# Recurrence gates in rounded terms with splits made early, and attention scores issued two parts at a time with tiles turned back four steps behind

## The chip, the cores and the metric

The kernel runs on 1 core of one Trainium2 chip. The metric is the time of one execution on the device, in microseconds. A core has TensorE (PE, with its weight loads as PEld), VectorE (DVE), ScalarE (ACT), GpSimd (POOL) and SyncE (SP); each takes its instructions in the order of its own queue, and semaphores tie the queues together.

## What is computed

Three transformer layers over 512 tokens of 1024 features: a hybrid of 8-head sliding-window attention and an RWKV recurrence, a sparse attention of 16 heads with three branches, and a block of dilated attention beside an LRU recurrence; each with feed-forward layers around it. What the change touches is this of the reference:

```python
# sliding window, 8 heads: band of two 128-key blocks, a sink per head
p = jnp.exp(s - m); p = p / (jnp.sum(p, -1, keepdims=True) + jnp.exp(sink - m))
# sparse attention, 16 heads: three branches, each a softmax of its own, summed under gates
return g_blk[..., 0, None] * o_cmp + g_blk[..., 1, None] * o_slc + g_blk[..., 2, None] * o_win
# LRU: two gates from the convolved input xc, per head of 256 channels
gate_x = jax.nn.sigmoid(jnp.einsum('bshi,hij->bshj', xh, w_x) + b_x)
gate_a = jax.nn.sigmoid(jnp.einsum('bshi,hij->bshj', xh, w_a) + b_a)
```

## The kernel before, in words

**Products.** Activations lie as features x tokens, 8 tiles of 128x512. Weights come in units of 8 blocks of 128x128 (one unit is one output tile of a product over 1024 features) into `raw`, issued by SP as slots come free (`SLOTS` = 6). ScalarE rounds a unit to `w_hi` (L123), VectorE makes the rest, `w_lo` (L130), and TensorE takes three rounded matmuls for each block (L155, L156, L157): high by high, high by low, low by high. Both engines prepare `AHEAD` = 4 units past the tile that they are at, and they do it in their own program order: in each tile of a product stands first the preparation (`act_ahead`, `dve_ahead`), then the tile's own work.

**The xr product and the convolution** (`lru_input`). For each of 8 tiles VectorE evicts the bank to `sq` (L1794), ScalarE makes the first term of a convolution (L1786, semaphore `first`) and VectorE three taps (L1797, `tap1` to `tap3`) into `xc`. Ahead of it, in ScalarE's queue, `load_lru` issues the loads of the gate weights `wx` and `wa` (L2464, L2465, semaphore `loaded`) and of the relative-bias table. After tile 5 TensorE picks relative biases (L1773), and after tile 6's taps VectorE makes the rows `rv` of them (`made`), which ScalarE writes to DRAM at h = 2 (`rel_vectors`).

**The gates** (`Scan`). The next product (`qkv0`, 9 tiles) is a host: ahead of each half tile, h = 0 to 17, stands a piece of other work. Gate t stands at h = 2, 4, .. 14 and 15 (L1851): per gate two weights by two blocks of `xc`, 4 unrounded matmuls of 128x512. Gate 0 shares banks 4 and 5 with tiles 4 and 5 of xr and waits for their eviction, gate 1 for `made`, later gates for the sigmoids of the gate before the last. ScalarE follows with two sigmoids (L1869, L1870), at h = 9 and 16 with powers and tangents (L1856, L1861), GpSimd with a multiplication (L1906), VectorE at h = 11 to 14 with squares (L1894, L1897).

**The attentions** (`paired_attention`) for the 8 heads (swa, 16 parts) and the 16 heads (nsa, 64 parts, two for each group, first the selected and then the local one). A part is scores of two heads, 64 rows each, side by side in the array (L1297), VectorE's bias with minimum (L1306), ScalarE's exponential (L1391), transposes on TensorE (L1317), ScalarE's copy (L1404), and matmuls with the values (L1330). VectorE settles a group (L1440 to L1458) out of its output bank: nsa has two banks, its last step a reduction over three branches (L1458); swa has one, since the recurrence's output (`guest`, L1123 to L1129, with L1143 and L1145 on ScalarE and L1174 to L1181 on GpSimd) takes the other. After four token tiles the finished tile is turned back (L1341), rounded (L1411) and its rest made (L1465). In step p TensorE's queue holds: scores of p + 2, transposes of p, the guest's matmul, value matmuls of p - 1, turning back of p - 2, and at the end an early part of the next product, 12 matmuls a step (L1204 to L1206). The other engines' queues follow the same steps.

## Time and profile before

| | us |
|---|---|
| median of 3 runs | 2758.2 |
| lowest and highest | 2757.69, 2758.71 |
| the profiled execution | 2757.42 |
| its span, first to last instruction | 2755.6 |
| TensorE busy in it | 2711.6 |
| VectorE, ScalarE, GpSimd busy | 1440.7, 1058.5, 36.4 |

The profile page gives busy times, the span in 40 slices, the chain of work that ended last and the costliest groups. The trace gives the single instructions: a row of a timeline has the start in us from the span's start, the duration, the engine, the line of the kernel, the operation, what it writes and reads, the shape, how many rows are merged into it, and in brackets the engine's idle time before it with what ended that. Matmuls overlap, so their cost is the distance between starts.

### The profile page before, as it was taken

The page shows a single profiled execution, that of the slowest core. Times are in us where ns is not written, and L with a number is a line of the kernel's source. Part 1 is how long each engine was busy: PE and PEld are TensorE (multiplying, and loading weights), DVE is VectorE, ACT ScalarE, POOL GpSimd, SP SyncE. Part 2 cuts the span into 40 slices and gives each one's busy share as a digit, 9 for nine tenths or more (in the row PEclk, how much of TensorE's full clock was granted, in tenths as well). Part 3 has the DMA queues.
Part 4 walks back from the last instruction along what each step waited for, and adds up shares of the span by engine and source line. Part 5 has one row for each costly group of instructions (what it writes and reads, how often), then busy time and mean ns, then how long its engine had stood idle before and what let it go on. Part 6 is the DMA issues. An engine that isn't in the chain of part 4 may idle for free.

```text
span 2755.6 us, 38503 instructions
## 1 busy us (share of the span) xinstructions
PE 2711.6 (98%) x16358; PEld 2248.7 (82%) x16358; DVE 1440.7 (52%) x2360; ACT 1058.5 (38%) x1604; POOL 36.4 (1%) x62
## 2 busy tenths in 40 slices
PE   9988999999999999999999999999999999999998
PEld 7787788888887788888888888877888788888887
DVE  6834576643625756756346443274634544654433
ACT  5534454332425654433234222245433422432221
POOL 0000200000000000000000000001000000000000
PEclk9999999999999999999999999999999999999999
DMA  4200122222531002322323332236222232223222
GB/s 161 90 4 3 53 87 98 100 94 98 158 104 39 1 1 100 100 97 95 100 77 107 99 99 93 100 116 129 82 81 87 71 100 98 87 99 99 93 99 69
DMA packets 68686, 238.85 MB, mean 87 GB/s; under 512 B 7800, under 2 KB 10360, under 8 KB 68004
## 3 DMA queue, kind: packets, MB, share of 16 engines
q1 hardware_dynamic: 62256, 220.80, 23.9%
q10 hardware_dynamic: 6260, 15.59, 2.5%
q8 instruction: 130, 2.13, 0.3%
q14 instruction: 40, 0.33, 0.0%
HBM read 228.23 MB, written 6.03 MB: 85 GB/s over the span
## 4 chain that ended last, share of the span: by engine, by line
PE 91%; DVE 4%; ACT 3%; issue 1%; POOL 1%; DMA 0%; ACTq 0%; another core or an unknown queue 0%; DVEq 0%; POOLq 0%
PE psum L155 23%; PE psum L157 23%; PE psum L156 23%; PE psum L1330 3%; PE psum L1297 2%; PE psum L1317 2%; PE psum L843 2%; PE psum L201 2%; PE psum L202 1%; PE psum L209 1%; PE psum L1851 1%; PE psum L177 1%; PE psum L178 1%; PE psum L176 1%; PE psum L1987 1%
## 5 line engine op out<-in xcount | busy, mean ns | idle before, releaser
L155 PE MATMUL psum<-x_hi,w_hi 128*128 128x512 f32 x2128 | 846.1, 398 | 0.7 <-DVE w_lo L130 0.7
L157 PE MATMUL psum<-x_hi,w_lo 128*128 128x512 f32 x2128 | 830.4, 390 | 0.0
L156 PE MATMUL psum<-x_lo,w_hi 128*128 128x512 f32 x2128 | 829.5, 390 | 0.0
L130 DVE TENSOR_TENSOR w_lo<-raw,w_hi 128x1024 fp32r<-128x1024 f32 x409 | 500.2, 1225 | 391.7 <-ACT w_hi L123 391.6
L123 ACT ACTIVATE w_hi<-raw 128x1024 fp32r<-128x1024 f32 x409 | 427.9, 1050 | 306.0 <-DMA raw<-w_down 83.9
L155 PEld LDWEIGHTS psum<-x_hi,w_hi 128*128 128x128 f32 x2128 | 400.0, 188 | 90.6 <-issue 5.7
L156 PEld LDWEIGHTS psum<-x_lo,w_hi 128*128 128x128 f32 x2128 | 400.2, 188 | 85.5 <-issue 5.0
L157 PEld LDWEIGHTS psum<-x_hi,w_lo 128*128 128x128 f32 x2128 | 399.8, 188 | 83.8
L157 PE MATMUL psum<-h_hi,w_lo 128*128 128x512 f32 x616 | 240.0, 390 | 0.0
L156 PE MATMUL psum<-h_lo,w_hi 128*128 128x512 f32 x616 | 240.0, 390 | 0.0
L155 PE MATMUL psum<-h_hi,w_hi 128*128 128x512 f32 x616 | 240.0, 390 | 0.0
L545 ACT ACTIVATE h_hi<-ht 128x512 fp32r<-128x512 f32 x88 | 55.6, 632 | 253.0 <-DVE ht L566 253.0
L157 PEld LDWEIGHTS psum<-h_hi,w_lo 128*128 128x128 f32 x616 | 115.7, 188 | 24.1
L155 PEld LDWEIGHTS psum<-h_hi,w_hi 128*128 128x128 f32 x616 | 115.7, 188 | 23.9
L156 PEld LDWEIGHTS psum<-h_lo,w_hi 128*128 128x128 f32 x616 | 115.7, 188 | 23.7
L553 DVE TENSOR_TENSOR sq<-psum,rn 128x512 f32<-128x512 f32 x88 | 60.7, 690 | 123.6 <-PE psum L157 114.7
L434 ACT ACTIVATE sq<-psum 128x512 f32<-128x512 f32 x49 | 29.2, 595 | 178.0 <-PE psum L157 163.4
L566 DVE TENSOR_TENSOR ht<-ffn_c,psum 128x512 f32<-128x512 f32 x88 | 60.5, 688 | 63.7 <-PE psum L157 61.1
L568 DVE TENSOR_TENSOR h_lo<-ht,h_hi 128x512 fp32r<-128x512 f32 x88 | 61.0, 693 | 61.4 <-ACT h_hi L545 61.4
L201 PE MATMUL psum<-x_hi,w_hi 128*128 128x512 f32 (+1 forms) x248 | 86.1, 361 | 4.8 <-ACT x_hi L286 3.1
L536 ACT ACTIVATE ffn_c<-sq,vec 128x512 f32<-128x512 f32 x44 | 35.9, 815 | 137.7 <-DVE sq L553 137.7
L202 PE MATMUL psum<-x_hi,w_lo 128*128 128x512 f32 (+1 forms) x248 | 83.1, 349 | 0.0
(412 smaller groups left out, 3298.5 us busy)
## 6 DMA issues: line engine op xcount, KB each, us to landing
raw<-w_up SPq DMA_DIRECT2D x88, 512.0 KB, 3.3
raw<-w_down SPq DMA_DIRECT2D x44, 512.0 KB, 3.3
raw<-w_f1up SPq DMA_DIRECT2D x44, 512.0 KB, 3.3
raw<-w_f2up SPq DMA_DIRECT2D x44, 512.0 KB, 3.3
raw<-w_qkv SPq DMA_DIRECT2D x36, 512.0 KB, 3.3
raw<-w_blend SPq DMA_DIRECT2D x28, 512.0 KB, 3.3
raw<-w_f1down SPq DMA_DIRECT2D x22, 512.0 KB, 3.3
raw<-w_f2down SPq DMA_DIRECT2D x22, 512.0 KB, 3.2
```

What stands on the lines that cost most here:

```text
L123: act.activation(self.w_hi[u % SLOTS][:], self.raw[u % SLOTS][:], ACT.Copy).then_inc(self.hi_done, 1)
L130: dve.tensor_tensor(self.w_lo[u % SLOTS][:], self.raw[u % SLOTS][:], self.w_hi[u % SLOTS][:].bitcast(F32), ALU.subtract).then_inc(self.lo_ ...
L155: pe.matmul(bank[:], hi, x_hi[:, kk], start=kk == 0, stop=False)
L156: pe.matmul(bank[:], hi, x_lo[:, kk], start=False, stop=False)
L157: mm = pe.matmul(bank[:], lo, x_hi[:, kk], start=False, stop=kk == kt - 1)
L201: pe.matmul(self.bank(g, t)[:, c], hi, x_hi[:, kk, c], start=n == 0, stop=False)
L202: pe.matmul(self.bank(g, t)[:, c], lo, x_hi[:, kk, c], start=False, stop=False)
L545: act.activation(h_hi[:, p], k.ht[p % 2][:], ACT.Copy).then_inc(high, 1)
L553: dve.tensor_tensor(pre[p % 2][:], gate[:], k.rn[:], ALU.mult).then_inc(k.bank_free, 1)
L566: dve.tensor_tensor(k.ht[p % 2][:], c[p % 2][:], val[:], ALU.mult).then_inc(k.bank_free, 1)
L568: dve.tensor_tensor(h_lo[:, p], k.ht[p % 2][:], h_hi[:, p].bitcast(F32), ALU.subtract).then_inc(low, 1)
L1330: mm = pe.matmul(out_bank[g % len(out_bank)][:, at * V:at * V + w], mem.pt[(c0 + count[(p, c)]) % 4][:, j * P:(j + 1) * P], values, start= ...
```

## The change

The gates: both operands of each gate pair j (gates 2j and 2j + 1) are split. ScalarE rounds the two weights' 128x512 slices (`round_weights`) and the two blocks of `xc` (`round_input`); GpSimd makes the four rests (`remainders`); TensorE multiplies in three rounded terms and waits for the rests (`split_lo`) in place of the load and `tap3`. Pair 0's weights are rounded in tile 0 of xr and its input in tile 2, pair 1's in tiles 3 and 4, pairs 2 and 3 at h = 6 and h = 10. The rounded copies lie in memory that is free at that time (under `acc`, `ln`, `r`, `ht`, `lru_ga`, `lru_gx`, `lru_e` and `z_even`).

The attentions: scores, minima, sink shifts and exponentials of parts p + 2 and p + 3 are both issued in even steps p; tiles are turned back four steps behind instead of two, and the early part of the next product starts one step later. In nsa the reduction over three branches becomes two additions on GpSimd out of a double buffer, and the value matmuls wait for the multiplication that empties the bank, no longer for the reduction.

```diff
+BEHIND = 4
...
-        done = p - 2
+        done = p - BEHIND
...
-                pe.wait_ge(taken, g0 + g + 1 - len(out_bank))
+                if steps == 3:
+                    pe.wait_ge(own, o0 + steps * (g + 1 - len(out_bank)))
+                else:
+                    pe.wait_ge(taken, g0 + g + 1 - len(out_bank))
...
-        for p in range(N + 2):
-            if p + 2 < N:
-                scores(pe, p + 2)
+        for p in range(N + BEHIND):
+            if p % 2 == 0:
+                for q in range(p + 2, min(p + 4, N)):
+                    scores(pe, q)
             if p == 0 and opening:
                 before(pe)
             if p < N:
                 guest.pe(pe, p)
             if 0 <= p - 1 < N:
                 mixes(p - 1)
-            back_to_features(p - 2)
-            if p >= N - 1:
+            back_to_features(p - BEHIND)
+            if p >= N - 4 + BEHIND:
                 head.pe(pe, 2)
...
+    def add_branches(pool, p):
+        g = parts[p].group
+        prod, ob = mem.prod[g % 2], mem.ob[g % 8]
+        pool.wait_ge(own, o0 + steps * g + 3)
+        pool.tensor_tensor(ob[:], prod[:, 0:P], prod[:, P:2 * P], ALU.add).then_inc(paired, 1)
+        pool.wait_ge(paired, g + 1)
+        pool.tensor_tensor(ob[:], ob[:], prod[:, 2 * P:3 * P], ALU.add).then_inc(taken, 1)
+
     def pool(pool):
         if not sinks:
+            for p in range(N):
+                if parts[p].last:
+                    add_branches(pool, p)
...
-                shift_sinks(pool, p + 2)
+        for p in range(N + BEHIND):
+            if p % 2 == 0:
+                for q in range(p + 2, min(p + 4, N)):
+                    shift_sinks(pool, q)
...
+        for p in range(N + BEHIND):
             if p < N:
                 copy(p)
-            features(p - 2)
-            if p + 2 < N:
-                exps(p + 2)
+            features(p - BEHIND)
+            if p % 2 == 0:
+                for q in range(p + 2, min(p + 4, N)):
+                    exps(q)
...
-                dve.tensor_tensor(mem.prod[:].rearrange("p (s v) -> p s v", v=HD), view[:, :, 0:HD],
+                if g >= 2:
+                    dve.wait_ge(taken, g0 + g - 1)
+                dve.tensor_tensor(mem.prod[g % 2][:].rearrange("p (s v) -> p s v", v=HD), view[:, :, 0:HD],
                                   coef.unsqueeze(2).to_broadcast([P, n, HD]), ALU.mult).then_inc(own, 1)
-                dve.wait_ge(own, at + 3)
-                dve.tensor_reduce(mem.ob[g % 8][:].rearrange("p (h v) -> p h v", h=2),
-                                  mem.prod[:].rearrange("p (s h v) -> p h v s", h=2, v=HD), AX.X, ALU.add).then_inc(taken, 1)
...
-                mins(dve, p + 2)
+        for p in range(N + BEHIND):
+            if p % 2 == 0:
+                for q in range(p + 2, min(p + 4, N)):
+                    mins(dve, q)
             if guest:
                 guest.dve(dve, p)
             if 0 <= p - 1 < N:
                 settle(p - 1)
-            lower(p - 2)
+            lower(p - BEHIND)
...
+            early(act, t)
             act.activation(mem.xc[:, t], k.sq[t % 2][:], ACT.Identity, bias=k.v("lconv_b", t),
                            scale=k.v("lconv_w3", t)).then_inc(first, 1)
...
+SPLITS = (6, 10)
...
+    def operands(self, j):
+        k, mem = self.k, self.mem
+        r, e = k.rounded, mem.e_rounded
+        ga, gx = mem.ga_rounded, mem.gx_rounded
+        if j % 2 == 0:
+            return [ga[:, KD - 2], gx[:, KD - 2]], [ga[:, KD - 1], gx[:, KD - 1]], (r[:, 4], r[:, 5])
+        if j == 1:
+            return [ga[:, KD - 4], gx[:, KD - 4]], [ga[:, KD - 3], gx[:, KD - 3]], (r[:, 6], mem.z_rounded[:, 8])
+        return [e[:, 4], e[:, 5]], [r[:, 2], r[:, 3]], (r[:, 6], mem.z_rounded[:, 8])
+
+    def round_weights(self, act, j):
+        mem, (_, _, wh) = self.mem, self.operands(j)
+        if j == 0:
+            act.wait_ge(mem.loaded, 32)
+        if j >= 2:
+            act.wait_ge(self.pair, 2 * j - 2)
+        for hi, w in zip(wh, (mem.wx, mem.wa)):
+            act.activation(hi, w[:, 4 * P * j:4 * P * (j + 1)], ACT.Copy).then_inc(self.w_high, 1)
+
+    def round_input(self, act, j):
+        mem, (xh, _, _) = self.mem, self.operands(j)
+        if j == KD // 2 - 1:
+            act.wait_ge(self.made, 2)
+        act.wait_ge(self.tap3, 2 * j + 2)
+        for kt in range(2):
+            act.activation(xh[kt], mem.xc[:, 2 * j + kt], ACT.Copy).then_inc(self.x_high, 1)
+
+    def remainders(self, pool, j):
+        mem, (xh, xl, wh) = self.mem, self.operands(j)
+        c = slice(4 * P * j, 4 * P * (j + 1))
+        for m, (hi, w, lo) in enumerate(zip(wh, (mem.wx, mem.wa), (mem.wx_lo, mem.wa_lo))):
+            pool.wait_ge(self.w_high, 2 * j + m + 1)
+            pool.tensor_tensor(lo[:, c], w[:, c], hi.bitcast(F32), ALU.subtract).then_inc(self.split_lo, 1)
+        for kt in range(2):
+            pool.wait_ge(self.x_high, 2 * j + kt + 1)
+            pool.tensor_tensor(xl[kt], mem.xc[:, 2 * j + kt], xh[kt].bitcast(F32), ALU.subtract).then_inc(self.split_lo, 1)
+
+    def early(self, act, t):
+        if t in (0, 3):
+            self.round_weights(act, t // 3)
+        if t in (2, 4):
+            self.round_input(act, t // 2 - 1)
...
             if t == 0:
-                pe.wait_ge(mem.loaded, 32)
                 k.tile_kept(pe, self.source, 5)
             if t == 1:
                 pe.wait_ge(self.made, 2)
             if t >= 2:
                 pe.wait_ge(self.ga, t - 1)
-            pe.wait_ge(self.tap3, t // 2 * 2 + 2)
-            for bank, w in zip(self.gate_banks(t), (mem.wx, mem.wa)):
+            j = t // 2
+            xh, xl, wh = self.operands(j)
+            pe.wait_ge(self.split_lo, 4 * j + 4)
+            for bank, hi, w in zip(self.gate_banks(t), wh, (mem.wx_lo, mem.wa_lo)):
                 for kt in range(2):
-                    o = ((t // 2 * 2 + kt) * 2 + t % 2) * P
-                    mm = pe.matmul(bank, w[:, o:o + P], mem.xc[:, t // 2 * 2 + kt], start=kt == 0, stop=kt == 1)
+                    c = slice((kt * 2 + t % 2) * P, (kt * 2 + t % 2 + 1) * P)
+                    low = w[:, 4 * P * j:4 * P * (j + 1)][:, c]
+                    pe.matmul(bank, hi[:, c], xh[kt], start=kt == 0, stop=False)
+                    pe.matmul(bank, hi[:, c], xl[kt], start=False, stop=False)
+                    mm = pe.matmul(bank, low, xh[kt], start=False, stop=kt == 1)
             mm.then_inc(self.pair, 1)
...
+        if h in SPLITS:
+            self.round_weights(act, 2 + SPLITS.index(h))
+            self.round_input(act, 2 + SPLITS.index(h))
...
+        self.remainders(pool, 0)
+        self.remainders(pool, 1)
         for t in range(KD):
+            if t in (3, 5):
+                self.remainders(pool, (t + 1) // 2)
             pool.wait_ge(self.gx, t + 1)
             pool.tensor_tensor(mem.gx[:, t], mem.gx[:, t], mem.xc[:, t], ALU.mult).then_inc(self.b, 1)
```

## Rows read from the trace of the kernel before

**Rows 1.** The page: engine busy (share) xinstructions; granted clock in 40 slices, in tenths.

```profile
PE 2711.6 (98%) x16358; PEld 2248.7 (82%) x16358; DVE 1440.7 (52%) x2360; ACT 1058.5 (38%) x1604; POOL 36.4 (1%) x62
...
PEclk9999999999999999999999999999999999999999
```

**Rows 2.** Timeline of TensorE around gates 0 and 1.

```profile
1848.10 1.88 PE L1851 MATMUL psum<-lru_xc,lru_wx 128*128 128x512 f32 x4
...
1851.76 0.40 PE L156 MATMUL psum<-x_lo,w_hi 128*128 128x512 f32 x1
...
1856.99 1.88 PE L1851 MATMUL psum<-lru_xc,lru_wx 128*128 128x512 f32 x4
```

**Rows 3.** By tile, the load of gate weight wa: start, time from issue to landing.

```profile
L2465 ACTq DMA_DIRECT2D lru_wa<-in_lru_a x1: 491/491/491, 1821.4 to 1821.4; - x1
...
DMA to landing us min/median/max: 12.4/12.4/12.4
```

**Rows 4.** The page, costliest groups: count | busy, mean ns | idle before.

```profile
L545 ACT ACTIVATE h_hi<-ht 128x512 fp32r<-128x512 f32 x88 | 55.6, 632 | 253.0 <-DVE ht L566 253.0
```

**Rows 5.** Timeline of ScalarE and VectorE in tiles 0 to 2 of xr.

```profile
1822.60 0.80 ACT L1786 ACTIVATE lru_xc<-sq,vec 128x512 f32<-128x512 f32 x1
...
1823.43 2.32 DVE L1797 SCALAR_TENSOR_TENSOR lru_xc<-sq,vec,lru_xc 128x511 f32<-128x511 f32 x3 [2.62 <-ACT lru_xc L1786]
...
1825.67 0.69 DVE L1794 TENSOR_TENSOR sq<-psum,rn 128x512 f32<-128x512 f32 x1
...
1829.47 1.22 DVE L130 TENSOR_TENSOR w_lo<-raw,w_hi 128x1024 fp32r<-128x1024 f32 x1
...
1830.61 0.68 DVE L1794 TENSOR_TENSOR sq<-psum,rn 128x512 f32<-128x512 f32 x1
```

**Rows 6.** Timeline, tile 6 on TensorE, the bias rows written, sigmoids of gate 4.

```profile
1831.63 0.50 PE L155 MATMUL psum<-x_hi,w_hi 128*128 128x512 f32 x1
...
1856.83 0.92 ACTq L1874 DMA_DIRECT2D rel_vectors<-rel_rv  x1
...
1885.77 1.06 ACT L123 ACTIVATE w_hi<-raw 128x1024 fp32r<-128x1024 f32 x1 [6.10 <-DMA raw<-w_qkv]
...
1894.46 0.69 ACT L1869 ACTIVATE lru_gx<-psum,vec 128x512 f32<-128x512 f32 x1
```

**Rows 7.** By line, GpSimd's multiplications of 128x512: duration in ns, min/median/max.

```profile
L1906 POOL TENSOR_TENSOR lru_gx<-lru_gx,lru_xc x8: 1277/1406/2277, 1861.1 to 1912.0; 128x512 f32<-128x512 f32 x8
```

**Rows 8.** Timeline, GpSimd and VectorE at the same time.

```profile
1897.33 1.75 POOL L1906 TENSOR_TENSOR lru_gx<-lru_gx,lru_xc 128x512 f32<-128x512 f32 x1 [0.83 <-ACT lru_gx L1869]
...
1897.85 1.78 DVE L1894 SCALAR_TENSOR_TENSOR lru_e<-lru_e,lru_ga 128x512 f32<-128x512 f32 x1
```

**Rows 9.** Timeline of TensorE in nsa, value matmuls ahead of scores and of transposes.

```profile
934.24 1.45 PE L1330 MATMUL psum<-nsa_vt,nsa_pt 128*128 128x65 f32 x12
...
935.62 0.76 PE L1297 MATMUL psum<-nsa_keys,z 64*128 64x287 f32 x4
...
1014.15 1.45 PE L1330 MATMUL psum<-nsa_vt,nsa_pt 128*128 128x65 f32 x12
...
1015.43 0.93 PE L1317 MATMUL psum<-const,nsa_p 128*128 128x128 f32 x7
```

**Rows 10.** By line, the transposes of nsa: duration in ns, min/median/max.

```profile
L1317 PE MATMUL psum<-const,nsa_p x336: 272/273/330, 850.0 to 1016.1; 128*128 128x128 f32 x168
```

**Rows 11.** Timeline, the reduction and the turning back of a tile.

```profile
893.70 0.59 DVE L1458 TENSOR_REDUCE nsa_ob<-nsa_prod 128x128 f32<-128x384 f32 x1
...
894.44 0.63 PE L1341 MATMUL psum<-const,nsa_ob 128*128 128x128 f32 x4 [0.25 <-ACT nsa_pt L1404]
```

**Rows 12.** Stretches, nsa: length, busy (x) of PE, PEld, DVE, ACT, POOL, clock, DMA.

```profile
850.00:1026.00 176.00, 174.26 (x1309) 140.06 (x1310) 118.43 (x506) 115.10 (x297) 0.00 (x0) 1.00 0.02 4
```

**Rows 13.** Timeline, swa: a sink row waited for, the guest waiting for ScalarE.

```profile
283.94 0.20 ACT L1396 ACTIVATE swa_es<-swa_es 128x2 f32<-128x2 f32 x1 [2.54 <-POOL swa_es L1363]
...
287.04 1.13 PE L1129 MATMUL psum<-rw_sg,z 128*128 128x512 f32 x2 [1.55 <-ACT rw_b L1143]
```

27 lines of the change are left out of this document (18 added, 9 removed).

## The prediction

> **What bounds the kernel now.** I read the page first: TensorE is busy for 98% of the span, and the granted clock is at its full level (2.4 GHz) in every slice [rows 1]. So an edit counts only by what it adds to or takes from TensorE's own queue: fewer or shorter matmuls, or a wait that TensorE has to sit out. I then read the timelines of the three places that the change touches. In the recurrence's gates the starts of successive instructions give the price of a matmul: from 1851.76 to 1856.99 lie 23 rounded ones, 0.227 us each, and from 1848.10 to 1851.76 one of these and eight passes of unrounded ones, 0.43 each [rows 2]. Durations don't, since matmuls overlap. In the same place ScalarE and VectorE feed TensorE by an order written out by hand, so their queues count too [rows 3 to 6]. In the two attentions the starts show no idle worth naming between parts, but dearer starts where matmuls of 64 rows begin and end, and one wait per tile turned back [rows 9 to 11].
>
> **Gates: the matmuls.** A gate issues 4 unrounded matmuls, each in two passes: 8 x 0.43 = 3.44 us [rows 2]. The change issues 12 rounded matmuls, 12 x 0.227 = 2.72 us. Eight gates: 8 x 0.71 = **-5.7 us**. Nothing covers or eats this; it is TensorE's own work.
>
> **Gates: the wait for the weights (the main term).** The rounding of the gates' weights now stands in ScalarE's queue in tile 0 of the xr product, ahead of the activation that begins that tile's convolution, and it first waits for both gate weights. Their loads are issued just before, the second at 1821.4, and it lands 12.4 us later, at 1833.8 [rows 3]; until now only TensorE waited for them, at gate 0, and found them there. ScalarE was at that point at 1822.6 [rows 5]. Behind it wait: the activation (L1786), then VectorE's three taps, and behind those in VectorE's queue the low part of weight unit 6 (L130 at 1829.47, ready at 1830.7), which TensorE needs for tile 6 from 1831.63 on [rows 5, 6]. Slack is 0.9 us. New times: loads 1833.8; two roundings, at 0.63 each as L545 [rows 4], 1835.1; first activation 1835.9; taps of 2.24 to 1838.2; eviction, activation and taps of tile 1 to 1842.0; unit 6 ready 1843.1. TensorE stands still some 11.5 us. Then the chain eviction, activation, taps, weight part, which took 4.94 us a tile (1825.67 to 1830.61) [rows 5], gets two roundings more in tiles 2, 3 and 4, 1.25 us each, 6.2 in all against 5.44 for a tile on TensorE (24 x 0.227). It stays in front: tile 5's eviction, which gate 0 needs since it shares its bank, ends at 1843.1 + 3 x 6.2 + 0.7 = 1862.4. Gate 0 starts then instead of at 1848.1: **+14.4 us**. TensorE's own work up to there (tile 6, tile 7 and a hosted tile, 16.3 us) ends at 1859.6, so up to 2.8 us of further slowness of TensorE are hidden here.
>
> The trace of before has no idle of TensorE this long and no half clock to read. The Trainium skill (TensorE: Matmul & The Clock Gate, Part 1) says that an idle TensorE is put back to 1.2 GHz until it has been busy again; nothing here shows it. By rows of the other level, a tile 6 wholly at half clock would take 5.4 us more, of which 2.8 are hidden, so the term is 0 to 2.6, and I take 0.
>
> **Gates: GpSimd beside VectorE.** Sixteen subtractions of 128x512 are new on GpSimd. Eight multiplications of that size took 1.28 to 2.28 there, median 1.41 [rows 7]. VectorE slows beside them: L1894 took 1.78 us where a tap of its size takes 0.75 (three in 2.32) [rows 5], and GpSimd's took 1.75 meanwhile [rows 8]. Four pairs fall into the chain of the last paragraph, and in each the second subtraction lies on VectorE's taps. At up to 1.0 us of VectorE each that is 0 to 4 us (6 if both of a pair meet it); I take three quarters of the one case seen: **+3.0**. The Trainium skill (GPSIMD Engine Reference, Key points) says that GpSimd shares its SBUF interfaces with VectorE instructions of two SBUF inputs; the trace agrees, by the 1.78.
>
> **Gates: two later waits.** Gate 1 needs the relative-bias rows that VectorE makes after tile 6. By the pace of the chain tile 6 was evicted at 1830.61 + 4 x 4.94 = 1850.4 [rows 5], and activation, taps and these rows took some 4.5 more: 1855, 2 us ahead of gate 1. From tile 5's eviction to their end VectorE needs 9.3 us; TensorE now reaches gate 1 only 8.2 after gate 0: **+1.0** (0 to 2). Gate 6 needs the last split. Its roundings stand behind gate 4's sigmoids in ScalarE, and these came only at 1894.46 to 1895.7, because ScalarE had waited until 1885.77 for a weight unit (the write of the bias rows, issued at 1856.83, shares the queues) and then did powers and tangents [rows 6]. One gate and its tile took 8.89 us (1848.10 to 1856.99) [rows 2], so TensorE wanted gate 6 at 1901.4. After: from gate 0's start, the weight unit is issued at +17.3 and lands, as before, some 20 later; sigmoids end at +46.8, GpSimd multiplies (1.3), then four subtractions of 1.3 to 2.0 [rows 7] end at +53 to +56. TensorE wants gate 6 at +50: **+4.5** (0 if the unit lands early, 10 if late and each subtraction takes 2). The split for gates 4 and 5 has 5 us to spare, and the bias loads behind the write may add 0 to 2 later; I take 0.
>
> **Sixteen-head attention (nsa).** The first matmul of 64 rows after the products starts 0.205 instead of 0.112 after the last pass, by which 12 passes take 1.38 ahead of scores and 1.28 ahead of transposes [rows 9]; and the first transpose behind scores takes 0.057 more than the rest, 0.330 against 0.273 [rows 10]. 62 parts come with such a pair of changes; two at a time leaves 31: 31 x 0.15 = **-4.6**. I assume that between two parts' scores no such gap appears (bound: 0 to -4.6). Turning back: L1341 came at 894.44, right behind the reduction that ends at 894.29 [rows 11], where the four passes before it, started at 893.63, would have let it start at 894.03. 7 of 8 tiles show it: 7 x 0.41 = **-2.9**; the last one, behind 4 steps of the early head, waits for nothing, and in its new place it has one step of 2.72 us to cover ScalarE's 0.60 and VectorE's 0.69. The first part's wait of 0.2 is covered too: **-0.1**. Is what feeds TensorE still in time? ScalarE is busy for 115 of 176 us and VectorE for 118 [rows 12]. In the tightest pair (t = 1) ScalarE has 0.60 + 1.06 + 1.41 us after the first transposes and VectorE 1.1 + 1.4; the second scores of the next pair want it 3.76 us after the last, and it is there at about 3.8. VectorE loses the reduction (0.594 x 32), which nothing waits for any more; GpSimd's two adds (between 0.20 for 128x2 and 1.28 for 128x512, taken as 0.5 each) are wanted 4 parts later. Sum **-7.6** (-8.5 to -4).
>
> **Eight-head attention (swa).** Seven pairs of changes fewer: 7 x 0.15 = -1.05. But there is one output bank, so products of a part wait for VectorE's settling of the last one, 0.95 us behind its start; with scores in every second step only, what stands between is one set of transposes (0.5). The guest's matmul (0.86) covers that up to step 11. In steps 13 to 16 it doesn't, and the early head no longer stands ahead of the last product: 3 x 0.4 + 0.45 against 0.43 + 0.33 before: +0.9. In the four steps behind a guest's variance the guest waits for ScalarE's logarithm, which now stands behind two parts' exponentials: 0.5 + 0.58 + 2 x 1.03 + 0.69 = 3.8 us after the scores, where TensorE comes at 0.5 + 0.86 + 0.9 + 0.5 = 2.76. 4 x 1.05 = 4.2 against 2.8 before (the longest, 1.55, at 287.04) [rows 13]: +1.4. The start, where the guest's mean now waits behind two parts' minima: +0.5. Sum **+1.8** (-1.5 to +5; GpSimd's sink rows, waited for 2.54 us at 283.94 [rows 13], now pass ahead of the guest's work, and speak for less).
>
> **The sum.** -5.7 + 14.4 + 3.0 + 1.0 + 4.5 - 7.6 + 1.8 = +11.4 us. The profiled execution took 2757.4 with a span of 2755.6; the median of the runs is 2758.2, 0.8 above it, and I add to the median: 2769.6.
>
> **Rivals.** (A) *The weights don't hold ScalarE*, because they land before it gets to them or VectorE has unit 6 ready by then. Then -5.7 - 7.6 + 1.8 = -11.5, 2746.7. It decides at 1.0 us of lateness of unit 6. Against it: load and wait are 11 us apart in the trace. (B) *The wait is there, but what follows it is free*: no contention, gate 1 and gate 6 in time: +2.9, 2761.1. For it: GpSimd and VectorE met in few places, and the write of the bias rows may give way sooner. (C) *The grouping doesn't do what it says*: two parts' scores in a row pay the 64-row change between them as well, and swa loses the same: +4.6 + 1.0, 2775.2. For it: inside one part's scores each pass already takes 0.1 us more than its columns.
>
> **Chances.** Forecast 0.70, A 0.08, B 0.14, C 0.08. About 0.2% (5.5 us) is what can be told from no change: below 2752.7 lies A, within it B, above 2763.7 the forecast and C. So faster 0.08, same 0.14, slower 0.78. The bounds of the unknown terms give -3 to +30 for the forecast; the range of 8 in 10 is 2755 to 2779.
>
> **What would show it.** In the profile after: L1786's first activation near 1835 minus what the attentions gave, and TensorE idle ahead of tile 6 for over 10 us (right), or none (A). A gate of 12 matmuls 2.7 us long. VectorE's taps beside GpSimd's subtractions well above 0.75 us each, or not (B). TensorE waiting for GpSimd at gate 6, 2 to 7 us. In nsa one start of 0.2 every second part, L1341 without a wait, 168 us for what took 176. In swa longer waits of L1129 and L1126 for L1143. Wrong would be above all a ScalarE that isn't held.

## The result and the profile after

The changed kernel took 2783.6 us (median of four executions, 2780.0 to 2787.1) against 2757.9 for the one before (four, 2757.5 to 2758.7): ratio 1.0093 [1.0081, 1.0106], 25.6 us slower. The forecast was 2769.6, range 2755 to 2779. The profiled execution is the slowest of the four: 2787.1, span 2785.0, 29.4 above the span of before.

The page of the changed kernel (to be held against [rows 1]; the last line adds the costliest group, with its idle):

```profile
PE 2710.6 (97%) x16390; PEld 2261.8 (81%) x16390; DVE 1424.0 (51%) x2328; ACT 1064.6 (38%) x1620; POOL 91.0 (3%) x142
...
PEclk9999999999999999999999999999999999999999
...
L155 PE MATMUL psum<-x_hi,w_hi 128*128 128x512 f32 x2128 | 842.9, 396 | 15.8 <-DVE w_lo L130 13.9
```

The row of the clock still says 9 in every slice: a slice is 70 us, too coarse for what follows. I laid the two traces side by side by matching TensorE's instructions in order; how far the start of a matched one has moved is the shift there. A stretch's share of the 29.4 us is what the shift grows over it:

| stretch (us in before) | recorded | measured | idle of TensorE: before, after |
|---|---|---|---|
| up to the eight-head attention, untouched code | 0 | +0.7 | |
| eight-head attention and its early head (swa), 250 to 330 | +1.8 | +4.5 | 5.7, 7.2 |
| sixteen-head attention and its early head (nsa), 846 to 1060 | -7.6 | +4.3 | 1.9, 11.0 |
| xr product and gates, 1800 to 2000 | +17.2 | +19.9 | 0.3, 21.0 |

Between the stretches the shift does not move. (In code that no run of this study changed it still moves by some 1 us from one execution to the next: at 250 us it lies between -1.5 and +0.9 in the experiments' profiles.) So 18 us are missing from the recorded sum, 11.9 of them in nsa.

**Xr and gates.** The timeline of the changed kernel, engines mixed, in order of time: ScalarE's wait in tile 0, tile 6 on TensorE, a tap row of VectorE beside GpSimd, gate 0, gate 6 (they answer to [rows 2, 3, 5, 6]):

```profile
1843.73 0.63 ACT L1872 ACTIVATE sq_to_r_rounded<-lru_wx 128x512 fp32r<-128x512 f32 x1 [11.63 <-DMA lru_wa<-in_lru_a]
...
1854.12 0.76 PE L155 MATMUL psum<-x_hi,w_hi 128*128 128x512 f32 x1 [12.98 <-DVE w_lo L130]
1854.69 0.63 PE L156 MATMUL psum<-x_lo,w_hi 128*128 128x512 f32 x1
1855.11 0.63 PE L157 MATMUL psum<-x_hi,w_lo 128*128 128x512 f32 x1
...
1856.50 3.22 DVE L1819 SCALAR_TENSOR_TENSOR lru_xc<-sq,vec,lru_xc 128x511 f32<-128x511 f32 x3 [1.92 <-ACT lru_xc L1808]
1856.56 1.83 POOL L1890 TENSOR_TENSOR lru_gx_rounded<-lru_xc,lru_gx_rounded 128x512 fp32r<-128x512 f32 x1
...
1875.30 0.50 PE L1922 MATMUL psum<-lru_ga_rounded,sq_to_r_rounded 128*128 128x512 f32 x1 [1.72 <-DVE sq L1816]
...
1877.93 0.39 PE L1924 MATMUL psum<-lru_gx_rounded,lru_wa_lo 128*128 128x512 f32 x1
...
1880.25 0.50 PE L155 MATMUL psum<-x_hi,w_hi 128*128 128x512 f32 x1 [1.93 <-DVE sq L1816]
...
1930.88 0.76 PE L1922 MATMUL psum<-lru_e_rounded,sq_to_r_rounded 128*128 128x512 f32 x1 [4.06 <-POOL sq_to_r_rounded L1890]
```

All that the prediction named is there: the wait for the load, the idle ahead of tile 6 (12.98), gate 0 behind tile 5's eviction and late by 1875.30 - 9.44 - 1848.10 = 17.8 us (9.44 being the shift on entry; recorded 14.4 + 3.0), the wait at gate 6 (4.06). What it left at nothing is the clock. Behind both idles the starts lie 0.43 us apart instead of 0.227 (1854.69 to 1855.11 in the rows), and the granted clock of the two stretches (length, busy of PE, PEld, DVE, ACT, POOL, clock, DMA) is:

```profile
1841.00:1858.90 17.90, 4.92 (x12) 3.79 (x12) 10.30 (x11) 6.41 (x9) 5.55 (x4) 0.62 0.14 56
1926.90:1934.00 7.10, 3.12 (x7) 2.48 (x8) 7.00 (x7) 1.79 (x3) 5.52 (x3) 0.77 0.81 147
```

TensorE had stood for 13.0 and 4.1 us and came back at 1.2 GHz. By the starts tile 6 was 2.3 us longer for it, gate 6 some 1.6. The Trainium skill (TensorE: Matmul & The Clock Gate, Part 1) says that an idle TensorE goes back to 1.2 GHz; the traces here agree for these two idles.

**Nsa.** The timeline in step 11, ahead of the first tile's turning back (answers to [rows 11]):

```profile
879.66 0.72 PE L1321 MATMUL psum<-const,nsa_p 128*128 128x128 f32 x5
879.74 2.34 ACT L1411 ACTIVATE nsa_p<-psum,nsa_mn 128x384 f32<-128x384 f32 x6
...
880.22 1.00 PE L1337 MATMUL psum<-nsa_vt,nsa_pt 128*128 128x65 f32 x8
...
881.87 0.45 POOL L1379 TENSOR_TENSOR nsa_ob<-nsa_ob,nsa_prod 128x128 f32<-128x128 f32 x1
881.93 0.81 ACT L1424 ACTIVATE nsa_pt<-psum 128x512 f32<-128x512 f32 x2
882.62 0.92 PE L1348 MATMUL psum<-const,nsa_ob 128*128 128x128 f32 x4 [1.40 <-ACT nsa_pt L1424]
```

Seven times 1.40 us. The turning back (L1348) needs its turn bank, which holds the first chunk of this step's transposes (879.66); ScalarE's copy of it (L1424) comes at 881.93, behind the second part's exponentials (L1411), the last of which starts at 881.76 (the row of six merges them). The sum of the branches isn't it: that of the tile turned back was made three steps earlier. The trace's record of the clock has half clock for 3.4 us directly behind three of the seven, and that can be priced: from one turning back to the next are 21.33 us where there is none (928.57 to 949.90), 22.98 where there is (905.60 to 928.57), and 21.53 in before. So half clock cost 1.64 each time, 4.9 us in all, more than the 4.3 that the stretch grew by.

The rows of before had this wait already. [rows 11] put the 0.25 us ahead of L1341 down to ScalarE's copy (L1404), not to VectorE's reduction; in the trace the reduction ends at 894.29 and the copy at 894.32. Without the reduction the wait would still have been there.

**Swa.** The stretch up to 299 us and the one behind it, in the changed kernel:

```profile
285.00:299.00 14.00, 11.59 (x84) 8.73 (x82) 9.45 (x39) 10.40 (x29) 8.78 (x13) 1.00 0.01 1
299.00:310.00 11.00, 11.00 (x47) 9.53 (x46) 3.16 (x13) 2.05 (x4) 0.00 (x0) 0.53 0.00 0
```

How much of the 4.5 us is the clock, e12 below tells, whose instructions are the same here and ran at full clock: up to some 300 us in the changed kernel the two traces keep one distance, and from there to the end of the half clock they part by 3.5 us. So 3.5 of the 4.5 are half clock, 1.0 is the change.

### The profile page after: what moved, and what is told of

It reads as the page before. It is cut to its first block, busy times and chain, and to the rows that moved or that the text cites. A ratio compares the mean times of both kernels' runs of the same rounds, so it can differ in the third digit from the quotient of the medians.

```text
span 2785.0 us, 38665 instructions
## 1 busy us (share of the span) xinstructions
PE 2710.6 (97%) x16390; PEld 2261.8 (81%) x16390; DVE 1424.0 (51%) x2328; ACT 1064.6 (38%) x1620; POOL 91.0 (3%) x142
## 4 chain that ended last, share of the span: by engine, by line
PE 88%; ACT 4%; DVE 4%; DMA 1%; issue 1%; POOL 1%; ACTq 0%; DVEq 0%
PE psum L155 22%; PE psum L157 22%; PE psum L156 22%; PE psum L1337 2%; PE psum L843 2%; PE psum L1301 2%; PE psum L201 2%; PE psum L202 1%; PE psum L1321 1%; PE psum L209 1%; PE psum L2067 1%; PE psum L177 1%; PE psum L178 1%; PE psum L176 1%; PE psum L849 1%
## 5 line engine op out<-in xcount | busy, mean ns | idle before, releaser
L1310 DVE CUSTOM_DVE_ANT_0 psum<-psum,nsa_table 128x31 f32<-128x31 f32 (+3 forms) x192 | 66.5, 419 | 32.7 <-PE psum L1301 32.5
```

Source lines behind the costliest of these rows:

```text
L1310: dve.tensor_tensor_reduce(out=slot[half][:, at:at + size], in0=slot[half][:, at:at + size], in1=table, scale=scale, scalar=least, op0=ALU ...
```

## The experiments

Times are medians over the executions; each ratio is to the kernel before run beside it (2757.2 to 2757.5). "Idle" is TensorE's in the stretch named.

### e1_attention and e2_gates: the change in two halves

The hunks in `paired_attention` and those for `mem.prod` and `BEHIND`, alone; and all the others, alone.

> Only the attentions' part of the change; the recurrence as before. The profile of the changed kernel is 9.4 us later than before when the xr product begins: 0.7 before the eight-head attention, 4.5 in it (nearly all of it in a half-clock stretch from 299 us on), 4.25 in the sixteen-head one. My theory: the two attentions cost that by themselves, so +4 to +9.5 us against before, the seven waits of 1.40 us ahead of the turning back (L1348) among it. Recorded prediction for this part: -5.8. Rival: the loss belongs to this one execution's clock, and without half clock the part is within 0.2% of before.

> Only the recurrence's part of the change; the attentions as before. Theory (this part's costs do not depend on the attentions): +20 us against before, as between the two profiles from the xr product to the end: 13.0 of stall ahead of tile 6, 1.9 of half clock behind it, 3.9 around gate 0, 5.5 at gate 6, less 5 to 6 of matmul time. Recorded prediction for this part: +17.2. Rival: TensorE arrives 9.4 us earlier here, so that the loads of the gates' weights meet other transfers; then the stall would differ from 13.0 by over 1 us.

Measured: 2762.6, 1.0019 [1.0009, 1.0030], +5.3 us; and 2776.3, 1.0071 [1.0056, 1.0086], +19.0. Together +24.3 of the 25.6: the halves add up. e1's eight executions lie between 2756.7, at a mean granted clock of 0.999, and 2767.0, at 0.994 (the profiled one). So the same instructions differ by 10.3 us with the half clock that an execution gets, and e1's theory and its rival are both in part right. In e2's profile the stretch from 1800 on has 20.9 us of idle and is 20.8 longer. The rival (another stall) fell: 12.45 against 12.98.

### e4_wait_only: the wait without the rounding

```
             k.tile_kept(act, g, t)
+            if t == 0:
+                act.wait_ge(mem.loaded, 32)
             act.activation(mem.xc[:, t], ...
```

> The kernel before with one thing added: ScalarE waits for both gate weights in tile 0 of the xr product, ahead of the activation that begins the convolution (no rounding, no split, no other change). The recorded working gives TensorE an idle of some 10.3 us ahead of tile 6 (11.5 less the two roundings of 0.63) and, as the chain then runs at its old pace of 4.94 us a tile against 5.44 on TensorE, +7.5 to +10.3 us in all without half clock (2.8 us hidden at gate 0 if gate 0 has slack). Rival (half clock counts): a half-clock stretch follows the idle as in the changed kernel, where TensorE lost 1.9 us behind it, and the whole is +10 to +12.5 us. Rival (no wait): below +1 us.

Measured: 2770.8, 1.0050 [1.0033, 1.0066], +13.5. In the timeline:

```profile
1842.48 0.77 PE L155 MATMUL psum<-x_hi,w_hi 128*128 128x512 f32 x1 [9.93 <-DVE w_lo L130]
1843.05 0.63 PE L156 MATMUL psum<-x_lo,w_hi 128*128 128x512 f32 x1
...
1845.61 0.43 PE L156 MATMUL psum<-x_lo,w_hi 128*128 128x512 f32 x1
1845.88 0.39 PE L157 MATMUL psum<-x_hi,w_lo 128*128 128x512 f32 x1
```

The rival (half clock counts) holds, if 1 us short by the median. The idle is 9.9 (recorded working: 10.3), the eight starts after it take 3.40 us instead of 8 x 0.227 = 1.82, and the shift grows by 11.45: 9.9 of idle and 1.5 of half clock, none of it given back at gate 0. A wait of 0.77 in the dilated attention, which before hasn't, brings the profile to 12.2. One added wait is half of the whole loss.

### e3_turn_back_at_3: the attentions' half, one step less

```
-BEHIND = 4
+BEHIND = 3
```

> Only the attentions' part, and the tiles turned back three steps behind instead of four. Theory 1 (ScalarE's order): the turning back four behind falls into an odd step, where the turn bank that it needs is freed by a copy that stands behind both parts' exponentials in ScalarE's queue (they end at 881.9, the copy at 882.5, L1348 starts at 882.62). Three behind falls into an even step, where that copy stands ahead of the exponentials: the seven waits of 1.40 us go, so do the half-clock stretches right behind three of them (1.1 to 1.8 us each), and the kernel is 10 to 15 us faster than with four, 3 to 8 us faster than before. Theory 2 (GpSimd's two adds, which end at 882.32 for another tile, or distance itself): one step less makes the waits as long or longer, and the time no better than with four.

Measured: 2756.5, 0.9998 [0.9989, 1.0008]; 6.1 us faster than e1. The wait of L1348 is gone, as theory 1 says, though GpSimd's adds have a step less. The gain of 10 to 15 us that it promised did not follow, for another wait came, seven times:

```profile
875.39 0.60 PE L1321 MATMUL psum<-const,nsa_p 128*128 128x128 f32 x4
...
875.59 0.60 ACT L1431 ACTIVATE x_hi<-psum 128x512 fp32r<-128x512 f32 x1 [0.46 <-PE psum L1348]
...
876.46 0.68 DVE L1485 TENSOR_TENSOR x_lo<-psum,x_hi 128x512 fp32r<-128x512 f32 x1
...
877.20 0.33 PE L1321 MATMUL psum<-const,nsa_p 128*128 128x128 f32 x1 [1.21 <-DVE x_lo L1485]
```

The next part has five transposes, in two chunks; the second wants the bank that the tile has just left, and VectorE frees it at 877.14. With 9.6 us of idle the stretch is still 1.9 shorter than before; without its idle it takes 212.1 - 9.6 = 202.5 against 214.0 - 1.9 = 212.1. So the grouping is worth 9.6 us, twice what was recorded. (The changed kernel gives the same: 4.3 less 9.0 of new idle less 4.9 of half clock is -9.7.)

### e5_nsa_odd_pairs, e6_adds_only and e9_nsa_odd_features: nsa alone, swa as before

e5 scores two parts together in odd steps and turns back two behind; e6 has the adds on GpSimd and nothing else; e9 is e5 with ScalarE's copy of the turned-back tile between the exponentials of the two parts.

```
+def scored(p, N, pairs):
+    if not pairs:
+        return range(p + 2, min(p + 3, N))
+    if p == 0:
+        return range(2, min(3, N))
+    return range(p + 2, min(p + 4, N)) if p % 2 == 1 else range(0)
...
-            features(p - behind)
-            for q in scored(p, N, pairs):
-                exps(q)
+            for n, q in enumerate(ahead):
+                exps(q)
+                if pairs and n == 0:
+                    features(p - behind)
```

> The sixteen-head attention alone is changed (the eight-head one and the recurrence as before): scores of two parts together, but in odd steps instead of even ones, tiles turned back two steps behind as before, adds on GpSimd. With three steps behind the stage lost 7 x 1.21 us ahead of the second transposes of a part (TensorE waits there for VectorE's L1485, which frees the turn bank) and was still 1.9 us shorter than before, so the grouping itself and the missing waits of L1341 would be worth 1.9 + 8.5 = 10.4 us. Theory (order of the copies on ScalarE and VectorE relative to the pair): in odd steps the copy that frees the turn bank stands ahead of the exponentials and the next part's transposes have one chunk, so no wait is left: 8 to 10 us faster than before. Rival (GpSimd's adds, 1.07 us behind L1478 where the reduction took 0.59): the turning back two steps behind now waits 0.4 to 0.9 us in each of seven tiles, 4 to 7 us faster. Recorded step: grouping -4.6, wait -2.9.

> The kernel before with one part of the change: the sum of the three branches of the sixteen-head attention on GpSimd (two adds of 128x128) instead of VectorE's reduction; order of scores and turning back as before. Theory (the turning back waits for the sum): the two adds end 1.07 us behind L1478, the reduction ended 0.59 behind it, so each of seven tiles waits 0.45 longer, +3 us (0.9 us of wait ahead of L1348 instead of 0.41). Rival (VectorE, relieved of 32 x 0.59 us, has its other work ready earlier): within 1 us of before or up to 2 us faster. The difference between this and the run with pairs in odd steps is the worth of the grouping alone; recorded: -4.6, by the run three steps behind about -7.5.

> As the run with pairs in odd steps, but ScalarE makes the first part's exponentials of a pair ahead of its copy of a turned-back tile, where it stood still for 0.57 us until TensorE had turned the tile and then copied for 0.60. Theory (ScalarE's order again): the 0.72 us ahead of the second scores of a pair (eight places, <- L1419) came from these 1.2 us; they go, and the sixteen-head attention gets 4 to 5 us shorter: 2750 to 2751.5. Rival (the exponentials of two parts are themselves too long for one pair's step): the waits stay within 0.2 us, 2755.

Measured: e5 2755.5, 0.9995 [0.9986, 1.0004]; e6 2760.8, 1.0014 [1.0004, 1.0023]; e9 2751.5, 0.9980 [0.9970, 0.9989], 5.9 us faster than before. Groups of instructions in nsa (busy, mean ns | idle ahead of them), one line each of before, the changed kernel, e6, e5 and e9:

```profile
L1341 PE MATMUL psum<-const,nsa_ob 128*128 128x128 f32 x32 | 5.0, 279 | 1.7 <-ACT nsa_pt L1404 1.7
```

```profile
L1348 PE MATMUL psum<-const,nsa_ob 128*128 128x128 f32 x32 | 5.5, 295 | 9.8 <-ACT nsa_pt L1424 9.8
```

```profile
L1358 PE MATMUL psum<-const,nsa_ob 128*128 128x128 f32 x32 | 5.0, 279 | 4.8 <-POOL nsa_ob L1388 4.8
```

```profile
L1311 PE MATMUL psum<-nsa_keys,z 64*128 64x415 f32 (+2 forms) x124 | 25.3, 485 | 5.2 <-ACT nsa_p L1419 5.2
```

```profile
L1311 PE MATMUL psum<-nsa_keys,z 64*128 64x415 f32 (+2 forms) x124 | 25.3, 485 | 0.2 <-ACT nsa_p L1419 0.2
```

e6's theory holds: it is 3.1 us longer in nsa and its idle 3.1 more. Taking the reduction off VectorE gives TensorE nothing where the tile is turned back soon. e5 missed its theory (8 to 10 us faster) and isn't clear of no change; it has the grouping, but ScalarE, in its queue, waits for the turned-back tile ahead of the exponentials; its rival named GpSimd's adds, and those cost nothing there (0.3 us of idle ahead of L1358). e9 takes that wait out, and its nsa is 6.7 us shorter than before. The three waits differ. In the change a short copy stands behind long work; in e3 the bank comes free only behind a chain, ScalarE's 0.60, then VectorE's 0.68, which stands 0.3 us behind other work; in e5 the long work stands behind a copy that waits for TensorE. What they share is an in-order queue whose order decides when a bank comes free.

### e12_eight_head_only

The grouping and the four steps behind in swa alone (conditions on `groups[0].slots == 1`; nsa as before).

> The eight-head attention's part alone (scores two parts at a time, tiles turned back four behind, early head accordingly); the sixteen-head attention with its reduction and the recurrence as before. Recorded: +1.8 (-1.5 to +5). In the profiles of the changed kernel, of the attentions' part alone, and of the one three steps behind, the stage was 4.5, 5.1 and 1.7 us longer than before, with 1.6 to 2.0 us more idle in each and half clock for 10.2, 10.2 and 3.4 us. Theory (the idle brings half clock, and that is most of the cost): +3 to +5 us in executions with a stretch of 10.2 us at half clock, +1.5 in those without; the executions differ by over 2 us. Rival (the waits cost by themselves, clock aside): +2 us in all of them.

Measured: 2758.9, 1.0004 [0.9994, 1.0013]. The stretch is 1.0 us longer, 2.5 more idle less 1.5 of saved work, and without half clock in the profiled execution. The waits for the one output bank grew by 1.9 (recorded 0.9), those for ScalarE's logarithm by 0.9 (recorded 1.4):

```profile
285.00:299.00 14.00, 12.07 (x85) 9.22 (x86) 8.68 (x35) 9.54 (x24) 7.74 (x10) 1.00 0.01 1
299.00:310.00 11.00, 10.33 (x57) 8.61 (x57) 2.54 (x10) 1.19 (x2) 0.00 (x0) 1.00 0.01 1
```

The executions differ by 2.6 us, at mean clocks of 0.998 and 0.999, so neither theory holds as written: the grouping with its waits costs 1.0 us by itself in the profile (the medians, +1.5, aren't clear of no change), and no execution shows the 4 to 5 us of the changed kernel. Why the same instructions with nearly the same idle (1.26 and 1.27 us the longest) were followed by 10 us at half clock in the profiles of the changed kernel and of e1 but not here, these runs don't settle.

### e7_gates_late, e8_gates_late_split8 and e11_lows_on_vector: where the splits stand

The recurrence's half alone, in all three. e8 adds the last split's move, e11 gives the subtractions for gates 0 to 3 to VectorE.

```
-            early(act, t)
             act.activation(mem.xc[:, t], ...).then_inc(first, 1)
+            early(act, t)
...
-        if t in (0, 3):
-            self.round_weights(act, t // 3)
-        if t in (2, 4):
-            self.round_input(act, t // 2 - 1)
+        if t in (3, 5):
+            self.round_weights(act, t // 4)
+        if t in (4, 6):
+            self.round_input(act, t // 2 - 2)
...
-SPLITS = (6, 10)
+SPLITS = (6, 8)
```

> The recurrence's part alone, with the weights for gates 0 and 1 rounded in tile 3 of the xr product and those for gates 2 and 3 in tile 5 (inputs in tiles 4 and 6), each behind the activation that begins the tile's convolution instead of ahead of it. With the roundings at tile 0 the part cost +19.0 us. Theory: the loads have landed by tile 3, so the 12.5 us idle ahead of tile 6 and the half clock behind it go; ScalarE idles for 3 to 4 us a tile behind that activation, so the roundings delay nothing and the idles of 1.7 and 1.9 around gate 0 go as well; left are -5.7 of matmuls and the idle of 4.2 at gate 6 with its half clock (1.5): within 2 us of before (-1 to +1 likeliest). Rival (the chain through ScalarE, GpSimd and VectorE is what counts, not the wait): gate 0 still waits for the remainders or VectorE's slower taps for 3 us or more, +3 to +7.

> As the run with late roundings, and the last split (gates 6 and 7) in step 8 instead of step 10: its roundings then stand behind gate 3's sigmoids, ahead of ScalarE's wait for a weight unit (7.34 us, until 1903.25) and ahead of the powers and tangents. Theory: the idle of 4.2 us ahead of gate 6 and the half-clock stretch behind it go: 5 to 6 us faster than the run with late roundings, -5 to -6 us against before. Rival (gate 6 is then held by its banks' sigmoids of gate 4, which ScalarE reaches at 1912): the idle shrinks by 2 us or less.

> As the run with late roundings and the last split in step 8, but the eight subtractions for gates 0 to 3 are VectorE's (two behind the taps of each of tiles 3 to 6) instead of GpSimd's. With GpSimd the three taps of such a tile took 4.12 to 4.15 us instead of 2.32, and the chain 6.8 to 6.95 us a tile instead of 4.94. Theory (contention is the price): two subtractions on VectorE cost 2 x 0.69 and the taps are back at 2.32, so a tile takes 6.3 us, and TensorE's idles ahead of tile 7 and gate 0 (5.3 us in all) shrink to 2.5 to 3.5: 2 to 3 us faster than with GpSimd. Rival (the chain's length is what counts, by whichever engine): no faster than with GpSimd (2765), for the work is now inside the chain.

Measured: e7 2766.4, 1.0036 [1.0024, 1.0048]; e8 2765.1, 1.0028 [1.0017, 1.0040]; e11 2762.0, 1.0017 [1.0008, 1.0027]. The idle ahead of tile 6 is gone in all of them; 1.6 us ahead of gate 0 and 3.7 ahead of the tile behind it remain in e7 and e8, 3.1 in e11. VectorE's taps of the same tile in e7, then in e11:

```profile
1843.54 4.15 DVE L1798 SCALAR_TENSOR_TENSOR lru_xc<-sq,vec,lru_xc 128x511 f32<-128x511 f32 x3 [0.89 <-ACT lru_xc L1786]
```

```profile
1842.12 2.32 DVE L1798 SCALAR_TENSOR_TENSOR lru_xc<-sq,vec,lru_xc 128x511 f32<-128x511 f32 x3 [0.88 <-ACT lru_xc L1786]
1844.37 0.68 DVE L1873 TENSOR_TENSOR lru_ga_rounded<-lru_xc,lru_ga_rounded 128x512 fp32r<-128x512 f32 x1
1844.97 0.68 DVE L1873 TENSOR_TENSOR lru_gx_rounded<-lru_xc,lru_gx_rounded 128x512 fp32r<-128x512 f32 x1
```

Two subtractions on GpSimd add 1.83 us to VectorE's taps; VectorE makes both in 1.28 by itself. So e7's rival holds in kind (+3 to +7 expected; 8.9 by the medians, 6.7 in the profile), and e11's theory, 3.1 us faster than e8. e8's theory, 5 to 6 faster than e7, fell: it was 1.3. The wait at gate 6 is gone in e7 already (why wasn't tested), so e8 can't show what the earlier split is worth. New in all three are waits of 3.5 to 3.9 us together in the dilated attention behind the gates. The next runs are about these.

### e10_gates_4_to_7, e13_gates_4_to_7_write and e14_write_wait_alone

e10: rounding for gates 4 to 7 alone (splits in steps 6 and 8). e13 adds the edit below; e14 is the kernel before with this edit alone. The wait guards `rel_rv`, which the powers of gates 6 and 7 overwrite.

```
-            if h == 16:
-                act.wait_ge(self.written, 16)
             first = 0 if h == 9 else 4
             for j in range(first, first + 4):
+                if j == 6:
+                    act.wait_ge(self.written, 16)
```

> The recurrence's part for gates 4 to 7 alone: gates 0 to 3 unrounded as before, splits in steps 6 and 8. Nothing of the change is left beside the xr product. Theory (all of the loss of the late version comes from GpSimd's subtractions beside VectorE's taps and the backlog that they leave): four gates at -0.71 each, -2.8 us, no new idle of TensorE, the waits of up to 2.9 us ahead of L2062 in the dilated attention gone as well. Rival (the later waits come from the splits for gates 4 to 7, whose subtractions slow VectorE down in the gates, or from ScalarE's four roundings each): 0 to +3 us.

> As the run with gates 4 to 7 rounded, and ScalarE's wait for the written bias rows stands behind the powers of gates 4 and 5 instead of ahead of them. In that run ScalarE was free at 1910.25 and stood until 1912.97, at nearly the time at which it went on in the kernel before (1912.76), although TensorE was 2.3 us ahead. Theory (the write's landing is a floor that does not move with TensorE): with table load and two powers (2.6 us) ahead of the wait, ScalarE's later work comes 2.5 us sooner, the waits ahead of L2067 and L2051 (2.6 us) go, and the gain of the matmuls stays: -2.5 to -3 us against before. Rival (ScalarE's backlog or the weight units hold the dilated attention): the waits stay within 0.5 us, no faster than before.

> The kernel before with that wait alone moved behind the powers of gates 4 and 5. Theory: there ScalarE had only 0.28 us of idle ahead of the table load, so nothing is won (within 0.5 us of before), which makes it the control. Rival (the moved wait itself speeds up the dilated attention, with or without the gates' gain): -1 us or more.

Measured: e10 2759.2, 1.0006 [0.9996, 1.0015]; e13 2754.0, 0.9987 [0.9978, 0.9996]; e14 2756.2, 0.9997 [0.9988, 1.0007]. ScalarE ahead of the powers, in before, e10 and e13:

```profile
1912.76 1.28 ACT L1856 ACT_TABLE_LOAD   x1 [0.28 <-issue]
```

```profile
1909.57 0.68 ACT L1929 ACTIVATE lru_ga<-psum,vec 128x512 f32<-128x512 f32 x1
1912.97 1.28 ACT L1915 ACT_TABLE_LOAD   x1 [2.72 <-issue]
```

```profile
1908.76 0.68 ACT L1929 ACTIVATE lru_ga<-psum,vec 128x512 f32<-128x512 f32 x1
1909.46 1.28 ACT L1915 ACT_TABLE_LOAD   x1
```

In e10 the shift falls from +0.66 to -2.25 by 1920 us, so the four gates give 2.9, and the dilated attention takes 2.6 back, because ScalarE doesn't get past the wait for the written rows before 1912.97. In e13 the waits are gone and the shift stays. e10's theory fell (+1.8 by the medians, not clear of no change), e13's holds. The write, issued at 1856.83 in before [rows 6], is a floor in time: by the packets of its queue it takes 51.0 to 52.4 us from its first one in the profiles of before, the changed kernel, e10, e13, e14 and e16, whatever TensorE does meanwhile. What TensorE gains behind the write's issue is lost until the wait is moved. e14, the control, wins 0.25 us in the touched stretch of its profile; its median is 1.0 faster, at the rival's bound and not clear of no change, so of e13's 3.2 us some may be chance. The profile puts the gain of e13 at 3.1.

### e15_gates_2_to_7 and e16_joined_4_to_7: do the parts add up?

e16 is e9 with e13; e15 rounds gates 2 and 3 too:

```
-SPLITS = (6, 8)
+SPLITS = (3, 6, 8)
```

> The sixteen-head attention of e9 and the recurrence with gates 2 to 7 rounded: the split for gates 2 and 3 in step 3 of the gates, 4 and 5 in step 6, 6 and 7 in step 8, the write's wait moved. Theory (splitting costs only where it meets the chain through VectorE's taps): six gates at -0.71, less at most 1 us at tile 7, whose taps meet no subtraction: -6.0 (e9) - 4.3 = 2747, 1.4 below e16. Rival (the subtractions of step 3 slow VectorE while it is behind with the taps of tiles 6 and 7 and with the bias rows, so gate 2 waits): no better than e16, or worse by up to 3 us.

> The sixteen-head attention of e9 (-6.0 us) and the recurrence of e13 (expected -2.8). Theory (the stages lie one behind the other on TensorE and share nothing): they add up, 2748.6 +- 1, 0.3% faster than before. Rival (TensorE arrives 6.7 us earlier at the xr product, where the loads of the weights for its gates are then met by others): the sum is missed by 2 us or more.

Measured: e15 2752.9, 0.9983 [0.9974, 0.9993]; e16 2748.4, 0.9965 [0.9952, 0.9978], 8.8 us faster than before: -5.9 and -3.2 add up. It is the fastest kernel of the study and has next to no idle of TensorE between 1800 and 2000 us. e15 is 4.6 us slower than e16, so its theory (1.4 faster) fell and its rival holds: gate 2 waits, and half clock follows:

```profile
1862.42 0.76 PE L1941 MATMUL psum<-lru_ga_rounded,sq_to_r_rounded 128*128 128x512 f32 x1 [4.04 <-POOL lru_gx_rounded L1902]
```

GpSimd needs 9.1 us from 1853.19 for one multiplication and the four subtractions of a split, more than there is between steps 3 and 6.

## Why the prediction was wrong, step by step

It had the sign and half of the size. The forecast's largest term was right; what put the time above the range is a term of nsa that failed, and half clock, which the sum took at nothing. By its own terms, for the profiled execution (29.4 against 11.4):

- **Wait for the weights, GpSimd beside VectorE: right.** Gate 0 came at +17.8 for +17.4 recorded, released by tile 5's eviction as the working has it; e4 showed the wait by itself. That up to 2.8 us of further slowness are hidden was right for the 2.3 us of half clock in tile 6, since gate 0 waited 1.72 more behind it. The subtractions cost VectorE's taps 0.9 a pair, 1.1 in tile 0, 3.8 in all for +3.0: ScalarE's roundings kept the first of each pair off them (where both meet them, as in e7, it is 1.83).
- **Matmuls of the gates: the size right, "Nothing covers or eats this" wrong in general.** -0.72 a gate in e10. Alone they run into the landing of the write (e10, e13).
- **Gates 1 and 6: +5.5 recorded.** Gate 1 waited for nothing; the tile behind gate 0 waited 1.93 us for VectorE's late evictions, which I had not listed. Gate 6: 4.06, and 1.6 of half clock. The stretch is 2.7 over the record. What the working puts down to shared queues are two in the trace (q10 for the write, q1 for the weights), but a weight unit issued between 1850 and 1915 us took 15.1 us to land, against 3.3 over the kernel (medians, before). (The stretch's growth of 19.9, less 20.7 of new idle, plus 5.7 of saved matmuls, leaves 4.9; 3.9 of that is half clock. The rest is that a wait costs a little more than its idle: the start at 1875.30 stands 2.11 behind the last, where the idle reads 1.72 and a matmul 0.227.)
- **Nsa: the step that failed.** The prediction forecast the turning back "without a wait" in its new place, and counted -2.9. It asked whether the tile's sum is ready, and not who frees the bank, although [rows 11] named that copy: four steps behind falls on an odd step, where the copy stands behind two parts' exponentials. Instead of taking 1.7 us of idle away it brought the stage 9.0 more, and 4.9 of half clock behind it. e3 and e5 moved the wait by moving the step; e9 removed it.
- **Grouping: mechanism right, size wrong.** -4.6 recorded, 9.6 us by e3 (7.1 by e5; the difference stays open). I had priced only the late start of the first 64-row matmul and the 57 ns by which one transpose is longer. But the start of the first transposes lies later than the columns of the last score pass ask for. Timeline of before, then of the changed kernel, same forms:

```profile
868.52 0.70 PE L1297 MATMUL psum<-z 64*128 64x256 f32 x4
869.16 0.44 PE L1317 MATMUL psum<-const,nsa_p 128*128 128x128 f32 x2
...
871.03 0.76 PE L1297 MATMUL psum<-nsa_keys,z 64*128 64x287 f32 x4
871.72 0.55 PE L1317 MATMUL psum<-const,nsa_p 128*128 128x128 f32 x3
```

```profile
873.29 0.70 PE L1301 MATMUL psum<-z 64*128 64x256 f32 x4
873.82 0.65 PE L1301 MATMUL psum<-nsa_keys,z 64*128 64x287 f32 x4
874.40 0.44 PE L1321 MATMUL psum<-const,nsa_p 128*128 128x128 f32 x2
```

  From the first pass to the transposes: 0.64 + 0.69 = 1.33 us apart, 1.11 together. The pairs of a tile save 0.17 to 0.22 so; with the 0.093 ahead of the scores and 0.05 on the second part's transposes that is some 0.33 a pair, 10 us for 31 pairs. Rival C (grouping gives nothing) is thereby refuted.
- **Swa: +1.8 recorded; +1.0 at full clock (e12), +4.5 with 3.5 of half clock.** Mechanism and size were near; the clock was not in the sum.
- **Half clock, "0 to 2.6, and I take 0": the mis-sized term of the whole.** I asked for it in one place, where it was hidden. Of the 18 us missing, some 11 are clock: 0.7 in untouched code, 3.5 in swa, 1.6 at gate 6 (tile 6's 2.3 were hidden) and 4.9 in nsa. The other 7 are nsa's: its idle is 12 us over the record, its grouping 5 better; the rest of swa came out 0.8 below the record, that of the gates 1.1 above. How much clock an execution loses is in part chance: against the medians 14 us are missing, 11.1 in the attentions' half and 1.8 in the gates'.

Rivals A and B fell by the 11.63 us of ScalarE's wait and by the wait at gate 6.

## What to carry to other kernels

Before grouping or delaying steps in a software pipeline, write down for each bank who frees it, and what stands ahead of that copy in its engine's queue at the new step's parity; here one step less was worth 6.1 us (e1 to e3), and one copy moved between two exponentials 4.0 (e5 to e9). A new consumer of a load must stand where the load has landed, and helper work on GpSimd where VectorE isn't on the chain. A gain counts only up to the next event that has its own time (here a DMA write), so look for that event behind every gain. And where a new idle of TensorE is forecast, give half clock behind it a term of its own, with a bound: here it was some 11 of the 18 us missed.

## What the runs showed of the hardware

- An idle of TensorE costs more than its length where half clock follows: 9.93 us cost 11.45 (e4), 12.98 cost 15.3. Half clock followed each of the nine idles of 3.1 to 13.0 us in these profiles (the changed kernel, e2, e4, e7, e8, e11, e15). Shorter idles are a lottery: the profiled execution of before has eleven of 0.9 to 1.9 us between 180 and 290 us and no half clock behind them, the changed kernel's nsa has it behind three of seven of 1.4 us, and eight executions of one kernel (e1) differ by 10 us.
- GpSimd's subtraction of 128x512 takes 1.27 us by itself and mostly 1.7 to 1.8 beside VectorE's taps; VectorE's own subtraction of that size takes 0.68. A row of three taps hides who pays: the 4.15 us of e7 are 0.75, 1.67 and 1.66, the 3.22 of the changed kernel 0.75, 1.65 and 0.75, so a tap that is issued beside a subtraction takes 0.9 more and the others nothing. The Trainium skill (GPSIMD Engine Reference, Key points) says that GpSimd shares its SBUF interfaces with VectorE and contends with its instructions of two SBUF inputs, as the taps are; the trace agrees, and shows that both sides pay.
